# Second block's attention: softmax probabilities and values kept as two fp32r halves, and their weighted sums made from three fp32r products in place of one fp32 product

## The reference

```
def attend(qg, keys, vals):
    s = jnp.einsum('bqkgd,bskd->bkgqs', qg, keys) * (HEAD_DIM ** -0.5)
    p = jax.nn.softmax(s, axis=-1).astype(vals.dtype)
    return jnp.einsum('bkgqs,bskd->bqkgd', p, vals)
```

## Time and profile before

| what | us |
|---|---|
| median of 3 runs | 3069.18 |
| the three runs | 3069.18, 3069.38, 3058.85 |
| the profiled execution | 3058.82 |
| its span, from the first to the last instruction | 3057.0 |
| TensorE busy | 2832.9 |
| VectorE busy | 1546.1 |
| ScalarE busy | 999.5 |

### The profile page before, as it was taken

The page is one execution under the profiler, slowest core; times in us unless marked ns, Lnnn a source line. Parts: engine busy times, 40 slices in busy tenths (PEclk is TensorE's granted clock), DMA queues, the critical chain, the costliest instruction groups (busy, mean ns, idle before and its releaser), DMA issues. The chain is left out here.

```text
span 3057.0 us, 35970 instructions
## 1 busy us (share of the span) xinstructions
PE 2832.9 (93%) x13890; PEld 2216.1 (72%) x13890; DVE 1546.1 (51%) x2122; ACT 999.5 (33%) x1689; POOL 476.3 (16%) x585
## 2 busy tenths in 40 slices
PE   7899999988548999999999999899989999989897
PEld 5666666667225877888888887688878877867785
DVE  6677878866554454115542426522243275546334
ACT  4444444444343334112221216511143222226321
POOL 2544444425011113000000002200010000002000
PEclk9999999999659999999999999999999999999999
DMA  5578777763123224223323323222223354451421
GB/s 194 182 300 316 281 302 295 303 226 139 37 88 111 95 99 153 85 103 129 117 96 138 128 95 134 107 80 95 75 91 105 125 176 147 150 181 59 158 96 55
DMA packets 111685, 447.17 MB, mean 146 GB/s; under 512 B 11440, under 2 KB 19760, under 8 KB 76208
## 3 DMA queue, kind: packets, MB, share of 16 engines
q1 hardware_dynamic: 111536, 445.16, 39.9%
HBM read 375.25 MB, written 69.86 MB: 146 GB/s over the span
## 5 line engine op out<-in xcount | busy, mean ns | idle before, releaser
L2734 PE MATMUL ps<-h_hi,w_hi 128*128 128x512 f32 x1600 | 576.9, 361 | 0.0
L2735 PE MATMUL ps<-h_lo,w_hi 128*128 128x512 f32 x1600 | 565.1, 353 | 0.0
L2736 PE MATMUL ps<-h_hi,w_lo 128*128 128x512 f32 x1600 | 561.4, 351 | 0.0
L386 PE MATMUL ps<-h_hi,w_hi 128*128 128x512 f32 (+1 forms) x1152 | 412.9, 358 | 35.7 <-DVE w_lo L345 35.7
L387 PE MATMUL ps<-h_lo,w_hi 128*128 128x512 f32 (+1 forms) x1152 | 412.0, 358 | 0.0
L388 PE MATMUL ps<-h_hi,w_lo 128*128 128x512 f32 (+1 forms) x1152 | 409.8, 356 | 0.0
L2734 PEld LDWEIGHTS ps<-h_hi,w_hi 128*128 128x128 f32 x1600 | 301.9, 189 | 49.8 <-issue 6.2
L2735 PEld LDWEIGHTS ps<-h_lo,w_hi 128*128 128x128 f32 x1600 | 301.7, 189 | 46.6 <-issue 6.2
L2736 PEld LDWEIGHTS ps<-h_hi,w_lo 128*128 128x128 f32 x1600 | 300.7, 188 | 43.5
L2512 DVE TENSOR_TENSOR w_lo<-raw,w_hi 128x2048 fp32r<-128x2048 f32 x64 | 146.4, 2287 | 311.4 <-ACT w_hi L2415 311.4
L386 PEld LDWEIGHTS ps<-h_hi,w_hi 128*128 128x128 f32 x1152 | 219.9, 191 | 70.7 <-DVE w_lo L345 38.7
(11 more groups left out here) (391 smaller groups left out, 4726.6 us busy)
## 6 DMA issues: line engine op xcount, KB each, us to landing
raw<-w_in SPq DMA_DIRECT2D x112, 1024.0 KB, 5.2
raw<-ada_w SPq DMA_DIRECT2D x96, 1024.0 KB, 8.3
raw<-w_out SPq DMA_DIRECT2D x48, 1024.0 KB, 5.0
proj<-xw SPq DMA_DIRECT2D x60, 384.0 KB, 2.6
xw<-proj SPq DMA_DIRECT2D x70, 256.0 KB, 3.4
xw<-proj SPq DMA_DIRECT2D x46, 384.0 KB, 3.3
xw<-resid SPq DMA_DIRECT2D x8, 1536.0 KB, 12.5
proj<-wide SPq DMA_DIRECT2D x32, 256.0 KB, 10.9
```

What stands on the lines that cost most here:

```text
L386: pe.matmul(a_[q], wh, h_hi[:, h0 + k, lo:hi], start=k == 0, stop=False)
L2734: pe.matmul(a_[q], wh, h_hi[:, k, a:b], start=k == 0, stop=False)
L2735: pe.matmul(a_[q], wh, h_lo[:, k, a:b], start=False, stop=False)
L2736: ins = pe.matmul(a_[q], wl, h_hi[:, k, a:b], start=False, stop=k == KC - 1)
```

## The change

The transposed probabilities and the transposed values are no longer read out as one float32 tile each. ScalarE copies `t_ps` into an fp32r tile (`pt_hi`, `v_hi`), and VectorE then subtracts that tile from `t_ps` and writes the remainder as fp32r (`pt_lo`, `v_lo`). `t_out` and `v_copied` are now counted up by VectorE's subtraction; ScalarE counts up two new semaphores, `p_high` and `v_high`. The tiles lie in `w_hi` and `w_lo`, which nothing else uses in this stage. `weighted(pr)` makes three fp32r matmuls for each block of 128 keys where it made one fp32 matmul. VectorE's order becomes `peak(g+2)`, `low(g)`, `v_low(1)` if g is `v_unit`, `result` if g is odd, `normalise(g+2)`, with `v_low(0)` ahead of the first.

```diff
-            pt = [xw[:, q * W:(q + 2) * W].rearrange("p (c n) -> p c n", c=6) for q in (2, 11)]
-            v_sb = wide[:, 2 * W:3 * W].rearrange("p (c d) -> p c d", d=P)
+            hi_flat, lo_flat = (w[:].rearrange("p a n -> p (a n)") for w in (w_hi, w_lo))
+            pt_hi, pt_lo = ([w[:, q * 2 * W:(q + 1) * 2 * W].rearrange("p (c n) -> p c n", c=6) for q in range(2)]
+                            for w in (hi_flat, lo_flat))
+            v_hi, v_lo = (w[:, 4 * W:5 * W].rearrange("p (c d) -> p c d", d=P) for w in (hi_flat, lo_flat))
...
-                            ins = pe.matmul(o_ps[pr % 2], v_sb[:, vc, :], pt[pr % 2][:, c, :], start=c == 0, stop=c == nch - 1)
+                            x_hi, x_lo = pt_hi[pr % 2][:, c, :], pt_lo[pr % 2][:, c, :]
+                            pe.matmul(o_ps[pr % 2], v_hi[:, vc, :], x_hi, start=c == 0, stop=False)
+                            pe.matmul(o_ps[pr % 2], v_hi[:, vc, :], x_lo, start=False, stop=False)
+                            ins = pe.matmul(o_ps[pr % 2], v_lo[:, vc, :], x_hi, start=False, stop=c == nch - 1)
...
-                        act.activation(v_sb, t_ps[:, 0:W].rearrange("p (c d) -> p c d", d=P), ACT.Copy).then_inc(v_copied.h, 1)
+                        act.activation(v_hi, t_ps[:, 0:W].rearrange("p (c d) -> p c d", d=P), ACT.Copy).then_inc(v_high.h, 1)
...
-                        act.activation(pt[pr % 2][:, 0:na, o:o + P], t_ps[:, 0:nk].rearrange("p (c q) -> p c q", q=P),
-                                       ACT.Copy).then_inc(t_out.h, 1)
+                        act.activation(pt_hi[pr % 2][:, 0:na, o:o + P], t_ps[:, 0:nk].rearrange("p (c q) -> p c q", q=P),
+                                       ACT.Copy).then_inc(p_high.h, 1)
...
+                    def v_low(kv):
+                        dve.wait_ge(v_high.h, v_high.at(kv + 1))
+                        dve.tensor_tensor(v_lo, t_ps[:, 0:W].rearrange("p (c d) -> p c d", d=P), v_hi.bitcast(F32), ALU.subtract
+                                          ).then_inc(v_copied.h, 1)
+
+                    def low(g):
+                        nk = of(g)[3]
+                        pr, o = g // 2, (g % 2) * P
+                        dve.wait_ge(p_high.h, p_high.at(g + 1))
+                        dve.tensor_tensor(pt_lo[pr % 2][:, 0:nk // P, o:o + P], t_ps[:, 0:nk].rearrange("p (c q) -> p c q", q=P),
+                                          pt_hi[pr % 2][:, 0:nk // P, o:o + P].bitcast(F32), ALU.subtract).then_inc(t_out.h, 1)
...
+                    v_low(0)
                     for g in range(total):
                         if g + 2 < total:
                             peak(g + 2)
+                        low(g)
+                        if g == v_unit:
+                            v_low(1)
                         if g % 2 and g > 2:
                             result((g - 3) // 2)
```

More of the change, by code:

```diff
@@ L201, in program @@
         low_ready, low_ready_v = count("low_ready"), count("low_ready_v")
+        v_high, p_high = count("v_high"), count("p_high")
         odd_copied, shifted = count("odd_copied"), count("shifted")
@@ L1758, in layer_attention @@
                          (neg_max, total), (exp_done, total), (p_ready, total), (t_ready, total), (t_out, total),
-                         (v_copied, 2), (m3, 2), (o_ready, total // 2),
+                         (v_copied, 2), (v_high, 2), (p_high, total), (m3, 2), (o_ready, total // 2),
                          (res_done, total // 2), (res_hi, total // 2), (res_lo, total // 2)):
```

## The result

The changed kernel takes 3098.6 us (median of 6 runs, 3093.2 to 3108.7) against 3069.3 us (6 runs, 3058.9 to 3071.4) for the kernel before. The ratio is 1.0109, with a 95% interval of 1.0088 to 1.0129: slower by about 1%. The forecast was 3090.7 us, in a range of 3069 to 3106: the direction and the range held, and the loss was 29.3 us where 21.5 were forecast.

A forecast was written before the change was run, and what follows sets the result against it. TensorE bounds the kernel before; the t_ps loop with the subtraction in it takes its place. 16.4 us in layer 0 and 5.1 in layer 1 make +21.5 on the 3069.2 us median: 3090.7 us, range 3069 to 3106.

The forecast's parts named there:

- The moved wait: Transposes of the next unit wait for VectorE's subtraction of t_ps, no longer for ScalarE's copy: 2.73 us, before about 1.8.
- the loop: One round of t_ps: transposes to copy 0.86, copy to subtraction 0.85, subtraction to next transposes 1.02; 2.73 us.
- a chain through VectorE's order: Layer 0, one head's first weighted sum to the next head's, subtraction queued behind a late peak: 17.69 us, +1.69 per head.
- The pairs and heads: Layer 1 pair 6.79 us against 6.48, +4.3 over 14 pairs; layer 0 +1.69 for each of 7 heads, +11.8.
- case D: TensorE's clock falls to 1.2 GHz after idle stretches in layer 0's heads: +14 on top, 3105 us; chance 0.13.
- The ends: Costs outside the repeating heads and pairs, at starts, tails and the middle v_low(1): 4.6 us in layer 0, 0.8 in layer 1.
- The end of layer 1: Last subtractions exposed, TensorE ending 2.73 - 1.77 later, behind weighted sums 0.50 and 0.48 us shorter: 0.
- Layer 0's tail: At the end of layer 0 two subtractions are exposed and a weighted sum is shorter: +1.1 us.
- The middle `v_low(1)`: Adds one subtraction to a chain that was partly hidden: +0.9 us in layer 0, +0.8 in layer 1.
- B: TensorE stays the bound, the t_ps round under 1.95 us: -16.6 us, 3052.6 us; chance 0.03.
- C: VectorE's order costs less in layer 0, a head paying only 0.62 us: +14 us in all, 3083 us; chance 0.16.
- E: Weight loads not hidden beside the products, a long weighted sum 5.0 us: +100 on top, 3190 us; chance 0.02.

The follow-up runs named there:

- x1: Changed kernel without VectorE's subtractions, all three products reading the high tiles: head 15.33 us, pair 6.05 us, 0.4% faster than the kernel before.
- x2: Changed kernel with one fp32 product again from a float copy, VectorE's subtraction kept: pair 7.32 us, head 18.77 us.
- x4: Changed kernel with each long weighted sum issued in two parts: pair 6.04 us, head 17.08 us, 0.4% slower than the kernel before.
- x5: Changed kernel with t_ps handed on in parts of 512 and 256 columns: pair 6.18 us, head 17.24 us, 28 us faster than the changed kernel.
- x3: Changed kernel with VectorE's low(g) ahead of peak(g+2): 39 us slower than the changed kernel by the medians, pair 8.12 us, head 21.1 us.
- x7: Changed kernel with layer 0's 256-key scores issued four times over: all heads but one 17.88 to 17.90 us, layer 0 3.4 us shorter.

## Why the prediction was right, and by how much it fell short

**The mechanism held.** The moved wait: the loop is 2.76 us (forecast 2.73), TensorE's way from even to odd transposes 4.13 (4.06) and back 2.76, in a pair of 6.88 (6.79). x1 and x2 take the change apart: the products alone save, the subtraction alone costs. x4 and x5 each remove one of the two conditions of the wait (too little work between two transposes, too long a loop). In layer 1 either brings the pair below that of the kernel before. In a head of layer 0 they take back 0.80 and 0.64 us of the 1.88. That is shown, not only argued.

For layer 0 the forecast had a chain through VectorE's order, of 17.69 us. The ordinary head of the changed kernel shows it link by link:

```profile
1882.28 0.96 DVE L1733 TENSOR_REDUCE stat<-ps 128x1 f32<-128x768 f32 x1 [0.26 <-PE ps L1609]
...
1883.46 0.91 ACT L1685 ACTIVATE xw<-ps,stat 128x768 f32<-128x768 f32 x1 [0.58 <-DVE stat L1735]
...
1884.48 0.16 DVE L1740 RECIPROCAL stat<-stat 128x1 f32<-128x1 f32 x1 [0.40 <-ACT xw L1685]
...
1885.21 0.95 DVE L1733 TENSOR_REDUCE stat<-ps 128x1 f32<-128x768 f32 x1
...
1886.39 0.90 ACT L1685 ACTIVATE xw<-ps,stat 128x768 f32<-128x768 f32 x1 [0.83 <-DVE stat L1735]
...
1887.41 0.17 DVE L1740 RECIPROCAL stat<-stat 128x1 f32<-128x1 f32 x1 [0.20 <-ACT xw L1685]
...
1888.15 0.95 DVE L1733 TENSOR_REDUCE stat<-ps 128x1 f32<-128x768 f32 x1
...
1889.20 0.95 DVE L1753 TENSOR_TENSOR w_lo<-ps,w_hi 128x768 fp32r<-128x768 f32 x1
...
1890.25 0.85 PE L1626 MATMUL ps<-ident_sb,xw 128*128 128x128 f32 x6 [1.65 <-issue]
...
1893.52 0.82 PE L1626 MATMUL ps<-ident_sb,xw 128*128 128x128 f32 x6
...
1894.37 0.81 ACT L1700 ACTIVATE w_hi<-ps 128x768 fp32r<-128x768 f32 x1 [1.97 <-PE ps L1626]
...
1895.21 0.96 DVE L1753 TENSOR_TENSOR w_lo<-ps,w_hi 128x768 fp32r<-128x768 f32 x1 [0.89 <-ACT w_hi L1700]
...
1896.28 0.41 PE L1626 MATMUL ps<-ident_sb,xw 128*128 128x128 f32 x2 [0.65 <-issue]
...
1900.16 0.96 DVE L1733 TENSOR_REDUCE stat<-ps 128x1 f32<-128x768 f32 x1 [0.27 <-PE ps L1609]
```

The lines are, in order: peak, exponential, reciprocal, peak, exponential, reciprocal, peak, subtraction, six transposes, then, behind a weighted sum and short scores, six transposes, copy, subtraction, two transposes, and, behind a weighted sum and scores, the next peak. From the first peak to the same peak of the next head is 17.88 us. Each link either waits for the one before it or stands directly behind it in its engine's queue, and the order is the forecast one. The 0.19 us missing in the forecast are 0.24 for the two weighted sums and 0.08 for the steps from subtraction to transposes, less 0.12 for the steps from transposes to sum. x3 shows with a run that this order matters.

**The pairs and heads: 2.7 of the 9.0 us that the two stages stand above the forecast.** They are 0.09 and 0.19 us longer than forecast. A product takes 0.12 us, the upper bound of the prediction, not 0.117; and the loop takes 0.03 more. The first product of a sum has 0.20 us to its successor, but this is no cost of its own, because it starts 0.08 us nearer to the transposes: 0.60 us in the changed kernel, 0.68 with the fp32 product behind the same wait (x2).

**The clock: 4.6 us net.** This is case D, which the prediction kept out of the likeliest, and its sign came: the mean granted clock of layer 0 is 0.93, under the 0.95 named there, and 0.97 before. The lower level cost 3.0 us in two heads and some 1.4 at the start of layer 0, where two loops took 3.45 and 3.46 us instead of 2.76. It cost 1.5 us in the last weighted sum of layer 1 (4.35 us to its `result`, 2.85 in x7 at full clock). Against this, layer 0's last sum had lost 1.7 us by it before the change and loses 0.4 now. All of this is of one profiled execution of each kernel. That it stayed this small, so that the median fell within the range, is in part luck.

**The ends: 1.8 us.** The start of layer 1 cost nothing, as forecast: from the first scores to those behind the first weighted sum there are 23.10 us (23.23 before), since the wait for head 1's queries absorbed the later start, 6.70 us of idle time having become 4.39. The end of layer 1, put at 0, cost 1.1: the last two loops stand bare, 0.98 us longer each, and the prediction took off both shorter sums there although one was already in its 14 pairs. Layer 0's tail cost 1.6 us without the clock (forecast 1.1), its start 2.7 (2.6). The middle `v_low(1)` cost 1.0 us in layer 0 and 0.9 in layer 1 (forecast 0.9 and 0.8). 2.7 + 4.6 + 1.8 is 9.1, against 9.0.

**The rivals.** B (TensorE stays the bound, 16.6 us less) needed the loop under 1.95 us. x1 is the kernel in which it holds, and it took 13.5 us less than the kernel before beside it. C fell: a head paid 1.88 us, not 0.62. D came for a part, as said. E fell on the spacing of 0.12 us. The Trainium skill's rule on weight loads ("TensorE: Matmul & The Clock Gate", section "The mechanism"; the prediction named the section behind it) would have them bare beside each product. The trace disagrees: it has 18 products with their loads in 2.24 us.

## What to carry to other kernels

Where one PSUM tile is handed round between a writer and its readers, add up the loop of one round before putting a second reader into it, and compare it with the least work that the writer has between two rounds, not with the mean: here it was 1.95 us in one of two, and a loop 0.81 us above that cost more than the 0.41 us by which the products shortened TensorE's way (3.25 to 2.84 us from transposes over the sum to the next scores). Two remedies helped here: to spread the writer's other work evenly between the rounds (x4), and to hand the tile on in parts (x5). On an in-order queue, put an independent instruction between a step and the one that needs the other engine's answer to it: the same instructions one place apart cost 39 us here, a part of it by the clock (x3).

## What the runs showed of the hardware

An fp32r product of 128x128 by 256 columns, with a weight load of its own, starts its successor 0.12 us later at the upper level of the clock; three of them replace one fp32 product of 0.43 us. The first one behind fp32 transposes stands 0.19 to 0.20 us ahead of its successor, in all sums of the changed kernel that ran at full clock. It starts earlier by as much, 0.60 us behind the transposes' start where an fp32 product behind the same wait starts 0.68 behind it (x2), so the sum pays nothing for it. Why the starts stand so was not tried.

A VectorE subtraction of 128x768 out of PSUM with an fp32r result takes 0.954 us, of 512 columns 0.686 and of 256 columns 0.414 (x5).

TensorE's granted clock fell to its 1.2 GHz level in layer 0's attention, with the engine busy 14.86 of the 17.88 us of an ordinary head, after idle stretches of 0.61 and 1.65 us with 1.3 us of work between them, and only in two of the heads with the same pattern. Each of the two falls cost 1.5 us.
